# Input projection in 256-column units, and two thirds of the output projection moved in among the mixer blocks

## What is computed

```python
z = rmsnorm(x, norm_g) @ w_in            # 1024 -> 2312 columns
# A: gelu(u) * (masked W_s @ rmsnorm(gelu(v))) + bias, blocks of 128 tokens
# B: attention in a window of 128 + own chunk of 64, 8 query heads, 2 kv heads, sinks, rotary on 16 dims
# C: mLSTM, 4 heads x 64: S = (q k^T) * exp(D - m_t); num = w_inter * (C q) + S v; C, n, m carried on
x = x + concat(A, B, C) @ w_out          # 1024 -> 1024
up = rmsnorm(x, ffn_norm) @ w_up         # 1024 -> 5632, causal convolution of width 3 over tokens
x = x + (gelu(c[:, :2816]) * c[:, 2816:]) @ w_down
```

## Time and profile before

| | us |
|---|---|
| median of 3 runs | 2800.8 |
| lowest, highest | 2800.26, 2801.57 |
| the profiled execution, whole | 2802.57 |
| its span in the profile | 2800.8 |
| mean granted clock of TensorE | 0.949 |
| PE busy | 2626.8 |
| DVE busy | 1423.2 |

### The profile page before, as it was taken

The page is one execution under the profiler, slowest core; times in us unless marked ns, Lnnn a source line. Parts: engine busy times, 40 slices in busy tenths (PEclk is TensorE's granted clock), DMA queues, the critical chain, the costliest instruction groups (busy, mean ns, idle before and its releaser), DMA issues.

```text
span 2800.8 us, 39846 instructions
## 1 busy us (share of the span) xinstructions
PE 2626.8 (94%) x15317; PEld 2463.0 (88%) x15317; DVE 1423.2 (51%) x2778; ACT 761.7 (27%) x1371; POOL 274.5 (10%) x390
## 2 busy tenths in 40 slices
PE   6999777999999999999999987779999999999998
PEld 5888555999999999999978875569999999999997
DVE  3110787346555555555531038763555555555555
ACT  4211544232222221222231134432322222122223
POOL 2100221230000000000240012213100000000003
PEclk7999877999999999999999997779999999999999
DMA  3222111211111111110012221130211111111101
GB/s 133 71 96 79 54 51 52 63 46 46 46 46 46 39 46 46 46 46 31 32 57 97 72 76 51 51 85 22 60 46 46 46 40 44 46 46 46 46 8 66
DMA packets 150892, 151.42 MB, mean 54 GB/s; under 512 B 8630, under 2 KB 136276, under 8 KB 148564
## 3 DMA queue, kind: packets, MB, share of 16 engines
q1 hardware_dynamic: 150740, 149.20, 16.6%
HBM read 123.62 MB, written 25.55 MB: 53 GB/s over the span
## 4 chain that ended last, share of the span: by engine, by line
PE 81%; DVE 10%; issue 2%; ACT 2%; POOL 1%; DVEq 0%; ACTq 0%; POOLq 0%
PE bank L256 26%; PE bank L257 25%; PE bank L258 25%; PE bank L802 2%; DVE prob L1519 1%; DVE mx L1498 1%; POOL nrm L294 1%; POOL actL L369 1%; DVE wLb L1628 1%; DVE cm L1528 0%; PE bank L691 0%; DVE vn L1488 0%; DVE Am L1526 0%; PE bank L345 0%; DVE G L1529 0%
## 5 line engine op out<-in xcount | busy, mean ns | idle before, releaser
L256 PE MATMUL bank<-actH,wHb 128*128 128x384 f32 (+1 forms) x1344 | 446.4, 332 | 1.1 <-POOL actL L369 1.1
L257 PE MATMUL bank<-actL,wHb 128*128 128x384 f32 (+1 forms) x1344 | 445.1, 331 | 0.0
L258 PE MATMUL bank<-actH,wLb 128*128 128x384 f32 (+1 forms) x1344 | 442.4, 329 | 0.0
L1633 DVE TENSOR_TENSOR xT<-bank,xT 128x384 f32<-128x384 f32 (+1 forms) x576 | 288.3, 530 | 208.7 <-PE bank L258 208.7
L256 PE MATMUL bank<-actH,wHa 128*128 128x384 f32 (+1 forms) x1056 | 349.3, 331 | 13.2 <-DVE upb L1665 7.1
L257 PE MATMUL bank<-actL,wHa 128*128 128x384 f32 (+1 forms) x1056 | 349.0, 331 | 0.0
L258 PE MATMUL bank<-actH,wLa 128*128 128x384 f32 (+1 forms) x1056 | 348.5, 330 | 0.0
L256 PE MATMUL bank<-wzH,actH 128*128 128x450 f32 (+1 forms) x720 | 276.8, 384 | 14.6 <-DVE wzL L1413 12.1
L257 PE MATMUL bank<-wzL,actH 128*128 128x450 f32 (+1 forms) x720 | 273.6, 380 | 0.0
L258 PE MATMUL bank<-wzH,actL 128*128 128x450 f32 (+1 forms) x720 | 273.5, 380 | 0.0
L1204 ACT ACTIVATE cv<-upb,convc 128x1090 f32<-128x1090 f32 x88 | 114.4, 1300 | 558.9 <-DVE upb L1677 558.9
(11 more groups left out here) (243 smaller groups left out, 4155.3 us busy)
## 6 DMA issues: line engine op xcount, KB each, us to landing
raw<-in_w_up SPq DMA_DIRECT2D x88, 512.0 KB, 3.9
raw<-in_w_down SPq DMA_DIRECT2D x44, 512.0 KB, 3.3
zb<-z_scratch SPq DMA_DIRECT2D x16, 1156.0 KB, 5.1
rawz<-in_w_in SPq DMA_DIRECT2D x8, 1800.0 KB, 7.3
z_scratch<-zst SPq DMA_DIRECT2D x64, 225.0 KB, 2.0
raw<-in_w_out SPq DMA_DIRECT2D x64, 128.0 KB, 2.7
xin<-in_x_prompt SPq DMA_DIRECT2D x8, 512.0 KB, 8.1
rawz<-in_w_in SPq DMA_DIRECT2D x8, 512.0 KB, 5.4
```

What stands on the lines that cost most here:

```text
L256: pe.matmul(out, aH, bH, start=first, stop=False)
L257: pe.matmul(out, aH, bL, start=False, stop=False)
L258: return pe.matmul(out, aL, bH, start=False, stop=last)
L1633: dve.tensor_tensor(xT[:, m, t0:t0 + w], bank[b][:, 0:w], xT[:, m, t0:t0 + w], ALU.add).then_inc(bank_free, 1)
```

## The change

- z has nine groups of 256 columns (the last 264). A unit is one group for one token tile, 81 in all, in four rotating banks. Groups 0 and 1 alternate by three tiles, in the first 18 units (those with gelu); groups 2 to 8 follow one by one. The first weights come in two pieces a group. Banks 4 to 7 are free of z. z_scratch and the load of zb stay.
- The parameter loads go to SP's queue between the stores of units 17 and 18, the table load to ACT behind unit 17, the transposes of gw and rows to PE behind unit 32, gwT and convc to ACT behind unit 33. zb of block 0 is loaded behind the store of unit 75.
- On PE the mLSTM uses bank 6 for all: dA, then q k^T (after A_used), W's transposes, numerator with the state update in columns 260 on, hc's transposes. dA now waits for blk_done of the block before; C q goes to bank 3, after the second ACT copy of pT; hc's transposes wait for cn_up.
- Slots `dense(b, 0)` to `dense(b, 7)` stand in each engine's `back`. By `W_AT`, 16 products, chunks 0 and 1 of w_out, run in them in banks 4 and 5: one in block 3, three in 4, four in 5, three in 6, three in 7, two in 8. Also in slots: DVE's adds, 12 splits of w_out on ACT (`W_HIGH`) and DVE (`W_LOW`), 16 squares on ACT, the sums on POOL (`ADDS`), the sum and mean of the norm of chunk 0. w_out is loaded and split twice (16 pieces, `N_WO`), SP issues the loads among those of zb.
- Behind the mixers `out_last` has the eight products of chunk 2; the norm of chunks 0 and 1 is under them.
- The loops over blocks and z groups are written out. SBUF is laid out anew: the z ring, its raw buffer and two pairs of w_out slots share one place, the mixers another.

The core of the diff:

```diff
-ZA, ZB = 512, 450
+ZG = (256, 264)
...
+        BLOCKS = [(i % 2, i, i // 2, DEC if i == NB else P, "first" if i == 0 else "last" if i == NB - 1 else
+                   "sample" if i == NB else "mid") for i in range(NTOK)]
+
+        def each_block(body):
+
+            for i in range(NTOK + 1):
+                body(BLOCKS[i - 1] if i else None, BLOCKS[i] if i < NTOK else None)
 
         Z_LOADS = (5, 4)
 
         def cols(i, r):
             return slice(SOFF, SOFF + DEC) if r == DEC else ds(i * P, P)
+
+        Z1, ZU, WU, WZ = 81, 81, 16, 11
+        MMS = WU + KT + 3 * (N_USE - KT)
+
+        def z_unit(u):
+
+            if u < 18:
+                s, t = u // 3 % 2, u // 6 * 3 + u % 3
+            else:
+                s, t = 2 + (u - 18) // NTOK, (u - 18) % NTOK
+            g = z_group(s)
+            return s, g * ZG[0], ZG[1] if g == 8 else ZG[0], t
+
+        def z_group(s):
+            return s
+
+        def z_last(s):
+
+            return (15, 18)[s] if s < 2 else 18 + NTOK * (s - 1)
+
+        def wz_at(s):
+            return 2 * s + 2 if s < 2 else s + 3
+
+        def z_stored(sp, l, u):
+            for i in range(3):
+                sp.wait_ge(z_st[i], 16 * (l * (ZU // 3) + (u - i) // 3 + 1))
+
+        W_AT = {(3, 5): 0, (4, 0): 1, (4, 2): 2, (4, 5): 3, (5, 0): 4, (5, 2): 5, (5, 3): 6, (5, 5): 7, (6, 2): 8, (6, 4): 9,
+                (6, 6): 10, (7, 0): 11, (7, 3): 12, (7, 5): 13, (8, 0): 14, (8, 2): 15}
+
+        def w_in_block(b, j):
+
+            return W_AT.get((b, j))
+
+        def w_unit(v):
+
+            c, m = v // KT, (v + v // KT * 4) % KT
+            return c, m, m if c == 0 or m >= 4 else KT + m
+
+        def wo_free(k):
+
+            return k - 3 if k < KT else k + 1
+
+        W_HIGH = {(3, 2): (0, 1), (3, 7): (2, 3), (4, 3): (4,), (4, 4): (5,), (4, 7): (6,), (5, 1): (7,), (6, 3): (8,),
+                  (6, 5): (9,), (6, 7): (10,), (7, 1): (11,)}
+        W_LOW = {(3, 3): 0, (3, 4): 1, (4, 0): 2, (4, 1): 3, (4, 4): 4, (4, 5): 5, (5, 0): 6, (5, 2): 7, (6, 4): 8,
+                 (6, 6): 9, (7, 0): 10, (7, 2): 11}
+        SQUARES = {(4, 0): (0, 0), (4, 2): (0, 1), (4, 4): (0, 2), (5, 0): (0, 3), (5, 2): (0, 4), (5, 4): (0, 5),
+                   (5, 5): (0, 6), (5, 7): (0, 7), (6, 4): (1, 0), (6, 6): (1, 1), (7, 1): (1, 2), (7, 2): (1, 3),
+                   (7, 5): (1, 4), (7, 7): (1, 5), (8, 2): (1, 6), (8, 4): (1, 7)}
+        ADDS = {(4, 1): (0, 1, 3), (5, 0): (0, 3, 5), (5, 1): (0, 5, 8), (6, 1): (1, 1, 2), (7, 0): (1, 2, 3), (7, 1): (1, 3, 5),
+                (8, 0): (1, 5, 6), (8, 1): (1, 6, 8)}
...
+                for u in range(Z1):
+                    store_z(u)
+                    if u == 5:
+                        next_wz(2)
+                    if u == 17:
+                        load_mixers()
+                        next_wz(3)
+                    for s in range(4, 9):
+                        if u == z_last(s - 3) + 2:
+                            next_wz(s)
+                    if u == 75:
+                        load_zb(0)
+                load_zb(1)
+                load_out(0)
+                load_out(1)
+                for i in (2, 3, 4):
+                    load_zb(i)
+                load_out(2)
+                load_out(3)
+                load_zb(5)
+                for k in range(4, 8):
+                    load_out(k)
+                load_zb(6)
+                load_out(8)
+                load_out(9)
+                load_zb(7)
+                load_out(10)
+                load_zb(8)
...
+                def w_products(v):
+
+                    c, m, k = w_unit(v)
+                    pe.wait_ge(S["blk_done"], l * 9 + (6 if c else 3))
+                    pe.wait_ge(wo_l, l * N_WO + k + 1)
+                    if v == 8:
+                        pe.wait_ge(ms_r, ms_at(2 * l + 1, 0))
+                    product(2 + m % 4, 4 + v % 2, c, M0 + v - 1 if v >= 2 else None)
+
+                def dense(b, j):
+
+                    if (b, j) == (6, 1):
+                        pe.wait_ge(bank_free, M0 + 7)
+                        norm_sum(pe, 2 * l + 1, 0)
+                    v = w_in_block(b, j)
+                    if v is not None:
+                        w_products(v)
...
+                    dense(i, 0)
+                    dense(i, 1)
                     if kind != "first":
-                        pe.wait_ge(S["cn_up"], b1 - 1)
-                    small(r)
-                    for h in range(4):
-                        m = pe.matmul(bank[4][0:r, h * P:h * P + r], qz[:, h, 0:r], ckT[:, h // 2, 0:r],
-                                      start=True, stop=True)
-                    m.then_inc(S["qk_r"], 1)
-
+                        pe.wait_ge(S["blk_done"], b1 - 1)
                     pe.wait_ge(S["dA_r"], b1)
                     if kind == "first":
                         pe.wait_ge(gwT_r, l + 1)
@@ -761,19 +855,19 @@
                     small(r)
                     pe.matmul(bank[6][:, 0:4 * r], ones[0:r, :], dA[0:r, 0:4 * r], start=True, stop=True).then_inc(S["A_r"], 1)
 
-                    if kind != "first":
-                        pe.wait_ge(S["blk_done"], b1 - 1)
                     pe.wait_ge(S["vn_r"], b1)
                     small(r)
                     for h in range(4):
...
+                    dense(i, 2)
+
+                    pe.wait_ge(S["A_used"], b1)
                     for h in range(4):
-                        m = pe.matmul(bank[5][0:r, h * 65:h * 65 + 65], qz[:, h, 0:r], CN[g][:, h // 2, :],
+                        m = pe.matmul(bank[6][0:r, h * P:h * P + r], qz[:, h, 0:r], ckT[:, h // 2, 0:r],
                                       start=True, stop=True)
-                    m.then_inc(S["int_r"], 1)
+                    m.then_inc(S["qk_r"], 1)
...
+                    if nch == 2:
+                        pe.wait_ge(S2["pTa_r"][1], c1)
+                    for h in range(4):
+                        m = pe.matmul(bank[3][0:r, h * 65:h * 65 + 65], qz[:, h, 0:r], CN[g][:, h // 2, :],
+                                      start=True, stop=True)
+                    m.then_inc(S["int_r"], 1)
+                    dense(i, 5)
...
+                    dense(i, 6)
                     if nx is not None:
                         scores(nx)
-
-                    pe.wait_ge(S["hc_r"], b1)
+                    dense(i, 7)
+
+                    pe.wait_ge(S["cn_up"], b1)
...
+                def out_last():
                     n = 2 * l + 1
-                    for c in range(3):
-                        for m in range(KT):
-                            e = c * KT + m
-                            if c == 0:
-                                pe.wait_ge(w_l, l * N_W + m + 1)
-                            product(m, e % 6, c, M0 + e - 5 if e >= 6 else None)
-                            if c and m == 0:
-                                norm_sum(pe, n, c - 1)
-                            if c and m == 1:
-                                norm_row(pe, n, c - 1)
+                    for j in range(KT):
+                        if j == 4:
+                            pe.wait_ge(sto_r, l + 1)
+                        pe.wait_ge(wo_l, l * N_WO + KT + j + 1)
+                        product(2 + j if j < 4 else j - 4 if j < 6 else j, (j + 2) % 6, 2, M0 + WU if j < 6 else M0 + WU + j - 5)
+                        if j == 0:
+                            norm_row(pe, n, 0)
+                        if j == 1:
+                            norm_sum(pe, n, 1)
+                        if j == 3:
+                            norm_row(pe, n, 1)
...
+                    if u == 17:
+                        act.preload_act_table_set("natural_log_exp_and_others")
+                    for s in range(2, 9):
+                        if u + 1 == z_last(s - 2):
+                            split_wz(s)
+                    if u == 33:
+                        act.wait_ge(par_tp, l * 2 + 1)
+                        act.wait_ge(init_r, l * INIT + INIT)
+                        t = bank[6][:, :].rearrange("p (h i) -> p h i", h=4)
+                        act.activation(gwT[0:64], t[0:64], ACT.Copy)
+                        act.activation(gwT[64:128, :, 64:128], t[64:128, :, 64:128], ACT.Copy).then_inc(gwT_r, 1)
+                        act.wait_ge(par_tp, l * 2 + 2)
+                        act.activation(convc[:, :], bank[7][:, 0:264], ACT.Copy).then_inc(conv_r, 1)
...
+                def dense(b, j):
+
+                    v = w_in_block(b, j)
+                    if v is not None:
+                        c, m, _ = w_unit(v)
+                        add_x(M0 + v + 1, 4 + v % 2, m, c)
+                    if (b, j) in W_LOW:
+                        split_out(W_LOW[b, j])
+                    if (b, j) == (6, 1):
+                        norm_mean(dve, 2 * l + 1, 0)
```

(21 more changed lines are left out.)

690 lines of the change are left out of this document (364 added, 326 removed).

## The result

The changed kernel takes **2810.3 us** in the median (2809.0 to 2815.3, six runs), the kernel before, beside it, 2800.5: a ratio of **1.0038, 95% interval 1.0025 to 1.005**. It is slower by 0.4%. Predicted were 2747 us, with 2712 to 2800 as the range: wrong in sign, and 10 us outside.

What follows compares the result with a forecast made beforehand. TensorE, busy 94% of the span, was taken to bound z and the feed-forward part, a dependent chain over four engines the mixers. Layers -61.8 us, z +11.4 and -4, in all -54: 2747 us median, range 2712 to 2800.

Steps and rivals of the forecast that it cites:

- the parameter loads: In z, the 22 loads' issue holds back SP's stores for 11 us, with 6 us to spare: +0.
- POOL's sums: In the mixers, sums of 0.985 us each fall where POOL waits for a load or for ACT: +0.
- the chain: Inside a mixer block, CN,qz wait for the last copy of pT: +1.1 us a block, +10 a layer.
- the norm fits: Behind the mixers, eight products, 3.6 us each, cover the norm of chunks 0 and 1; POOL needs at most 2.96 a product.
- z's width: In z, 256-column matmuls at 0.119 us each instead of 450-column ones: +5.7 us a layer, +11.4 in all.
- Rival D: In z, the weight load sets the distance of narrow matmuls: 2865 us (0.04) or 3016 (0.01); chance 0.05.
- The head of z: At the start of z, unit 0 needs half the weights and splits: -4 us, between 0 and -12.
- z to the mixers, first product: After z, ACT's table load and copies move into z: -2.6 us a layer; first product's weights are ready behind mixers: -3.1.
- dA just in time: In a mixer block, dA waits for blk_done, takes about a microsecond and is ready when read at 411.31.
- Sixteen products: Moved into the mixers, 4.2 us each: -67.2 a layer behind, +33.8 inside; slot 5 costs 4.2, slot 6 2.3.
- Rival C: In the mixers, products and chain run one after the other, in slots 0 and 2: 2835 us; chance 0.10.
- E: In the mixers, w_out's parts land late and products wait in TensorE's queue: 2771 us; chance 0.05.

Runs made afterwards that it cites:

- e1: Changed kernel with one load of w_in (group 3) issued ahead of the 22 parameter loads in SP's queue; 2790.0 us, ratio 0.9976 to the kernel before.
- e8: On e1: in layer 1 ACT evacuates z units 0 to 3 among its steps for chunk 1's norm; ratio 0.9967 to the kernel before.
- e3b: Changed kernel with matmuls of the sixteen products, adds, squares, sums and eight w_out splits cut down, leaving mainly the chain; mixers 227.8 us against 265.2.
- e5: On e1: CN,qz matmuls go back behind vn, into bank 4, and the products share bank 5; ratio 0.9893 to the kernel before.
- e7: On e1: hc's transposes in bank 4, products in bank 5 alone, dA without the wait for blk_done; ratio 0.9964 to the kernel before.
- e4: Changed kernel with POOL's fourteen sums of squares among the mixers cut to one column; mixers 252.9 us against 265.2.
- e6: On e1: seven of POOL's fourteen sums a layer moved behind its power for vn; ratio 0.9937 to the kernel before.

## Why the prediction was wrong

The forecast for the span was -54 us, measured +6.6. Four steps of the prediction failed: the parameter loads (+0, measured 19.0 us), POOL's sums (+0, measured some 18), the chain (+20, measured some 38), and "the norm fits" behind the mixers (10.6 us too cheap). The 61 us between forecast and measurement, by its own steps (both layers):

- **z's width** (+11.4): right in kind, too dear. e1's z runs 852 matmuls in 100 us, 0.1174 us each instead of 0.119, and those of the last group, of 264 columns, start 0.121 apart: 8 x 0.1174 + 0.121 = 1.060 against 1.052, +1.8 us a layer. That is 8 us in the change's favour. Rival D is out: the loads' records still last 0.188 us, and they hide, also behind a product this narrow. The rule of the Trainium skill on row groups that stood with D (TensorE: Matmul & The Clock Gate, "What overlaps and what doesn't") does not hold here.

```profile
100.00:200.00 100.00, 100.00 (x852) 100.00 (x851) 9.64 (x9) 22.94 (x43) 2.83 (x8) 1.00 0.36 109
```

- **The head of z** (-4): -0.4 in layer 0 (what e1's z is longer by, 1.4 us, less the width), as the norm of the later chunks sets it. In layer 1 it was not looked at, and is +6.2: four banks of narrow units hold 11 us of work (4 x 24 x 0.117), where the kernel before had six wide ones for 33 us, so TensorE runs into ACT's squares. e8 shows what lies behind them: chunk 2's sums.
- **"SP's 22 parameter loads: +0"**: failed, 19.0 us (e1: 8.7 and 10.3). The step priced what the 22 issues hold back among the stores, and e1 shows that this was right: 11.9 us of hold, no stop. It left out the one load of w_in that the change had put behind them.
- **z to the mixers, first product**: -3.1 and -3.4 a layer, predicted -2.6 and -3.1. Right.
- **The chain** (+1.1 us a block, +10 a layer): too cheap. What is left of the mixers' 58.2 us without products, sums, adds and most splits is 23.8 a layer (6.5 in blocks 0 to 2, and e3b's 17.3), some 19 without the four splits of 1.22 us. e5 shows the term: CN,qz wait for ACT's last copy of pT, while the first value products need only the one before it, and stand ahead of them. The prediction priced the matmuls (1 to 1.8 us) and not this wait of some 0.5 us; both are undone with 9 us a layer, in spite of the lost bank. "dA just in time" holds at the full clock (e7 wins nothing); at the low one dA's matmuls last 2.07 us and VectorE waits 0.59. In blocks 1 and 2 the chain costs 1.5 us a block in e1, inside the prediction's 0.9 to 1.8, and 3.7 in the changed kernel: the difference is where the low clock falls. How much of the cost in blocks 3 to 8 is the clock stays open.
- **Sixteen products** (+33.8 with adds and splits): too dear, if not by much. Measured 14.1 for the matmuls, 11.2 for adds, squares and most splits and some 5 for the other four splits, about 30; the first figure is net of the clock that the products bring back. Slot 5 was seen rightly as the dear one, and slot 6 as cheaper; the difference is 2.7 us, not 1.9, the clock included. Rival C has a grain of truth: in slot 0 the product ends 2.2 us behind the block before, and VectorE waits 0.8 us.
- **"POOL's sums: +0"**: failed, 9.1 us a layer in the blocks that hold them, 18 in all (e4; e6 wins back 4.5 a layer with half of them moved). Only POOL's own time was looked at, not what its steps do to VectorE's. The Trainium skill has the rule (SBUF — State Buffer, "SBUF: two separate sides"): the two engines share a pair of ports to SBUF, which one instruction holds alone, and a VectorE step with two SBUF inputs is among those that block or are blocked. The trace agrees: dn, hc and mixA x uT (0.96 us instead of 0.43) wait for the sum, nd<-nd,bank (0.42 us) and Wt<-bank,Am (0.68), which read PSUM, last as long beside a sum as without one. That reading would have put the +0 in doubt before the run.
- **Behind the mixers** (-67.2, "the norm fits"): 5.3 us a layer less, with two waits of 3.1 and 3.9 us in layer 0. POOL's steps were added up as if alone; beside VectorE's splits a sum takes 1.85 us.

In sum: -7.7 (width), +3.6 and +6.2 (heads), +19.0 (the load), +32.4 (mixers: 16.2 a layer), +10.6 (behind), -3 (small ones): 61. The mixers' 16.2 are some 9 for the chain and 9 for the sums, less 4 for the products, which were priced too dear, and 2 that the forecast had credited to the clock. Block by block the forecast was 5.3, 7.2, 8.8, 6.8, 7.7 and 4.6 us for blocks 3 to 8, and measured are 5.0, 10.1, 12.6, 6.6, 12.0 and 5.3: it fits in blocks 3, 6 and 8, and is 3 to 4 us short in blocks 4, 5 and 7. No rival had these mechanisms: C and D put the cost into TensorE's products and weight loads, E into w_out's loads.

## What to carry to other kernels

When a batch of loads is moved in a queue, follow the first transfer that stands behind it, not only what is stored around it: one line here is worth 0.6%. An engine off the chain is free only if its steps do not hold up those of the chain's engine: here POOL's work on SBUF belongs beside steps of VectorE that read PSUM, or where VectorE waits. And work that is slid into a dependent chain belongs where it runs beside the busiest engine's own steps (slot 6), not where that engine already waits (slot 5): the same four products, 1% of the whole.
